# Scaling a tile inside the product that turns it: a diagonal of reciprocal norms in place of a VectorE pass

## What is computed

```python
h = rmsnorm(x, attn_norm)                    # y = x * rsqrt(mean(x*x) + eps) * gain
proj = h @ w_in                              # 1024 x 3584
o_a = dilated_mixture_attn(...)              # three groups of heads, dilations 1, 4, 16
o_b = sink_swa_gqa(...)                      # window of 128 with sinks
o_m = memory_attn(m_q, mem, mem_norm, ...)   # rmsnorm(mem) @ w_mem_kv, then attention
gates = sigmoid(h @ w_gate + b_gate)
merged = sum of gates[i] * (o_i @ w_o_i)
x = x + merged @ w_out                       # called x1 below
x = x + conv_ffn(rmsnorm(x, ffn_norm), w_up, conv_w, conv_b, w_down)
```

## Time and profile before

| | us |
|---|---|
| median of 3 runs | 1708.54 |
| lowest and highest | 1705.82, 1713.55 |
| the profiled execution | 1709.16 |
| its span in the trace | 1707.4 |
| PE busy | 1648.7 (97%) |
| DVE busy | 927.6 (54%) |
| POOL busy | 968.6 (57%) |
| ACT busy | 664.9 (39%) |
| mean granted clock of PE | 0.993 |

### The profile page before, as it was taken

One profiled execution on the slowest core, in us unless ns is written; L12 is line 12 of the kernel. 1 busy time (PEld: TensorE's weight loads), 2 busy tenths in 40 slices (PEclk: granted clock), 3 DMA queues, 4 the chain that ended last, 5 costly groups with the idle time before them and its releaser, 6 DMA issues.

```text
span 1707.4 us, 22529 instructions
## 1 busy us (share of the span) xinstructions
PE 1648.7 (97%) x8518; PEld 1353.1 (79%) x8518; DVE 927.6 (54%) x1327; ACT 664.9 (39%) x1172; POOL 968.6 (57%) x729
## 2 busy tenths in 40 slices
PE   7999989989899989999999999999999999999999
PEld 5887878868778768888888887788888888788887
DVE  7455342457875672224554367888888888522001
ACT  5555565545544333335212325343343434322110
POOL 5643656542312477775245548999999997222221
PEclk9999999999999999999999999999999999999999
DMA  5113011111110323332655502222222322443311
GB/s 219 38 59 103 2 38 41 38 26 33 44 38 8 86 80 114 121 100 77 182 158 183 191 38 62 87 84 89 75 74 87 94 80 103 163 146 128 140 50 62
DMA packets 132904, 151.07 MB, mean 88 GB/s; under 512 B 15349, under 2 KB 95933, under 8 KB 132797
## 3 DMA queue, kind: packets, MB, share of 16 engines
q1 hardware_dynamic: 132364, 149.62, 27.4%
q10 hardware_dynamic: 432, 0.01, 0.0%
HBM read 116.98 MB, written 32.62 MB: 88 GB/s over the span
## 4 chain that ended last, share of the span: by engine, by line
PE 59%; POOL 3%; DVE 2%; DMA 1%; ACT 1%; issue 0%; SPq 0%; DVEq 0%; ACTq 0%; POOLq 0%
PE ps L2805 24%; PE ps L2890 13%; PE ps L2140 11%; PE ps L2180 6%; PE ps L2196 3%; PE ps L2131 1%; DMA w_raw<-in_w_out_dram 1%; POOL wo L1862 1%; POOL f_lo L2646 0%; PE ps L2189 0%; DVE ffn_area L2763 0%; POOL f_lo L1867 0%; DVE attn_lo L2755 0%; DVE t_all L2673 0%; POOL ffn_area L1880 0%
## 5 line engine op out<-in xcount | busy, mean ns | idle before, releaser
L2646 POOL TENSOR_TENSOR f_lo<-ffn_area,f_hi 128x1024 fp32r<-128x1024 f32 x85 | 200.8, 2382 | 20.3 <-ACT f_hi L2533 20.3
L2678 POOL TENSOR_TENSOR attn_lo<-ffn_area,attn_lo 128x512 fp32r<-128x512 f32 x44 | 58.5, 1330 | 194.4 <-ACT attn_lo L2595 194.3
L2805 PE MATMUL ps<-t_all,f_hi 128*128 128x512 f32 x528 | 164.1, 392 | 1.9 <-DVE t_all L2673 1.6
L2533 ACT ACTIVATE f_hi<-ffn_area 128x1024 fp32r<-128x1024 f32 x85 | 80.2, 946 | 188.8 <-PE ps L2805 178.4
L1867 POOL TENSOR_TENSOR f_lo<-ffn_area,f_hi 128x1024 fp32r<-128x1024 f32 (+1 forms) x42 | 99.9, 2381 | 73.6 <-ACT f_hi L1715 73.6
L2805 PE MATMUL ps<-act_hi,f_hi 128*128 128x512 f32 x336 | 133.3, 397 | 4.6 <-POOL f_lo L2646 4.6
L688 POOL TENSOR_SCALAR head_rstd<-head_ss 128x8 f32<-128x8 f32 (+2 forms) x42 | 11.0, 262 | 217.9 <-DVE head_ss L979 217.9
L2805 PE MATMUL ps<-act_hi,f_lo 128*128 128x512 f32 x336 | 132.3, 394 | 0.0
L2805 PE MATMUL ps<-act_lo,f_hi 128*128 128x512 f32 x336 | 131.2, 391 | 0.0
L1277 PE MATMUL ps<-w_hi,act_hi 128*128 128x512 f32 (+1 forms) x320 | 122.5, 383 | 5.3 <-DVE w_lo L504 2.6
L2805 PEld LDWEIGHTS ps<-t_all,f_hi 128*128 128x128 f32 x528 | 98.9, 188 | 24.5 <-DVE t_all L2673 1.6
(11 more groups left out here) (314 smaller groups left out, 4586.5 us busy)
## 6 DMA issues: line engine op xcount, KB each, us to landing
ffn_area<-in_w_up_dram SPq DMA_DIRECT2D x44, 512.0 KB, 5.2
gate<-gates SPq DMA_DIRECT2D x24, 512.0 KB, 3.7
ffn_area<-in_w_gate_dram SPq DMA_DIRECT2D x23, 512.0 KB, 5.2
z<-attn_out SPq DMA_DIRECT2D x22, 512.0 KB, 2.6
ffn_area<-in_w_down_dram SPq DMA_DIRECT2D x22, 512.0 KB, 4.1
ffn_area<-z SPq DMA_DIRECT2D x44, 256.0 KB, 2.9
gates<-ffn_area SPq DMA_DIRECT2D x40, 256.0 KB, 2.1
attn_out<-in_x_dram SPq DMA_DIRECT2D x16, 512.0 KB, 6.3
```

The source lines that it names most:

```text
L2533: act.activation(part_place(p, part, f_hi, first_hi), part_source(p, part), ACT.Copy).then_inc(w_hi_done, 1)
L2646: pool.tensor_tensor(part_place(p, part, f_lo, first_lo), part_source(p, part), part_place(p, part, f_hi, first_hi).bitcast(F32), ALU.subt ...
L2678: pool.tensor_tensor(z_lo[:, m % 2, :], z_raw[:, m % 4, :], z_hi[:, m % 2, :].bitcast(F32), ALU.subtract).then_inc(z_lo_done, 1)
L2805: ins = pe.matmul(out, w, a, start=(start and k == 0 and i == 0), stop=(stop and k == 3 and i == 2))
```

## The change

The scaled tile is no longer written. DVE multiplies the unit matrix by the reciprocal norms, each row by its own, which gives a diagonal matrix of 128x128; for x and the memory it goes to a new tile `x_diagonal`, for x1 to the first 128 columns of the buffer in which the scaled tile stood. PE multiplies the unscaled tile as stationary operand by this diagonal as the moving one, in a plain float32 product in place of the transpose: the result is the turned tile with each column scaled. `x_diagonal` exists once, so its next writing waits until both halves of the tile before are turned (`x_turned`), the first one for `ident_ready`. The order of the instructions on every engine is the same as before: PE and DVE have as many, in the same places.

```diff
+        x_diagonal = sb("x_diagonal", [P, P])
...
             def x_scale(n):
                 dve.wait_ge(x_rstd, n + 1)
-                dve.tensor_scalar(x_slot[n], x_slot[n], row_rstd[:, n:n + 1], None, ALU.mult).then_inc(x_scaled, 1)
+                if n >= 1:
+                    dve.wait_ge(x_turned, 2 * n)
+                else:
+                    dve.wait_ge(ident_ready, 1)
+                dve.tensor_scalar(x_diagonal[:], ident[:], row_rstd[:, n:n + 1], None, ALU.mult).then_inc(x_scaled, 1)
...
                 for k in range(4):
-                    ins = pe.transpose(x_half(n, h)[:, k * P:(k + 1) * P], x_slot[n][:, (4 * h + k) * P:(4 * h + k + 1) * P],
-                                       ident[:])
+                    ins = pe.matmul(x_half(n, h)[:, k * P:(k + 1) * P], x_slot[n][:, (4 * h + k) * P:(4 * h + k + 1) * P],
+                                    x_diagonal[:], start=True, stop=True)
                 ins.then_inc(x_turned, 1)
...
                 dve.wait_ge(x1_rs, 2 * t + 2)
-                dve.tensor_scalar(staged[:, t % 2, :], x1[:, t, :], rstd[:, t:t + 1], None, ALU.mult).then_inc(x1_scaled, 1)
+                dve.tensor_scalar(staged[:, t % 2, 0:P], ident[:], rstd[:, t:t + 1], None, ALU.mult).then_inc(x1_scaled, 1)
...
                 for k in range(NK):
-                    ins = pe.transpose(turned(t)[:, k * P:(k + 1) * P], staged[:, t % 2, k * P:(k + 1) * P], ident[:])
+                    ins = pe.matmul(turned(t)[:, k * P:(k + 1) * P], x1[:, t, k * P:(k + 1) * P], staged[:, t % 2, 0:P],
+                                    start=True, stop=True)
                 ins.then_inc(x1_turned, 1)
```

## The result

The changed kernel takes **1720.39 us** (median of 6 runs, 1718.14 to 1721.74), the kernel before 1709.14 us in the runs beside it (6 runs, 1705.82 to 1713.55): a ratio of **1.0066, 95% interval 1.0053 to 1.0078**, slower by 11.25 us. The prediction was 1721.3 us (1716 to 1727) and slower. Other traces of the same two programs have spans of 1706.6 and 1707.0 us (before) and 1715.5 us (after), so a step of the ledger that is under 1 us can be chance where nothing else bears it out.

A forecast was written before the change was run, and what follows sets the result against it. PE, busy 97% of the span, was taken as the bound. Terms 0.8 + 0.9 - 0.1 - 1.5 + 5.5 + 7.1 gave +12.7 us, so 1721.9, lowered 0.6 to the median: 1721.3 us, range 1716 to 1727.

The forecast's parts named there:

- The price: Every turn on PE: a tile's eight plain products take 1.70 us against 0.79 for transposes, 0.91 us more.
- tiles 4 to 9: Half turns of x and the memory from 41.54 to 110 us: six times 0.91, +5.5 us.
- Rival C: All turns: plain products cost four times the transpose, 2.37 us more a tile, +40 us, 1749 us; chance 0.03.
- rival D: All turns: diagonal product costs PE what a transpose does, leaving only DVE's gain, 1707 us; chance 0.05.
- Tile 0: Kernel's start: slower first turn, partly hidden by ACT's square, delays the first projection and the w_lo wait; +0.8 us.
- Rival A: Near 18 us: w_lo slips ahead of POOL, removing the 2.2 us wait and half clock; 1717.6 or 1716.6; chance 0.12.
- Tile 1: Turn between 18 and 22 us: full price paid, half-clock stretch assumed to last as long; +0.9 us.
- Tiles 2 and 3: Ahead of the key copy at 41.54 us: PE's extra work fits into its wait; -0.1 us instead of +1.8.
- The clock behind the key copy: PE's half clock from 43 to 46 us goes as waits shrink; -1.5 us, bounds 0 and -1.5.
- x1: Eight x1 turns at 0.91 us, less a 0.2 us wait: +7.1 us, nothing hiding the last turn.
- Rival B: Clock does not recover: +14.2 us, 1722.8, or 1724.7 with nothing hidden at tiles 2 and 3; within forecast's 0.80.
- DVE's gain in all: Scalings of 18 tiles: 0.5 us less each, 9 us of DVE in all, almost none on the path.

The follow-up runs named there:

- x alone: Kernel before with only x and the memory scaled by the diagonal product, x1 left as it was; 1713.29 us, 1.0024.
- DVE alone: Kernel before with DVE making only the small diagonals, while PE transposes unscaled tiles and the multiplication by the norms is left out; 1704.91 us, 0.9978.
- tiles 1 to 3: Kernel before with the diagonal product for tiles 1, 2 and 3 of x only; 1709.76 us, 1.0001.
- the second repeat of the kernel before: Kernel before, unchanged, run again for a third trace; 1708.84 us.
- x1 alone: Kernel before with only x1 scaled by the diagonal product, x and the memory left as they were; 1713.56 us, 1.0031.
- one with doubled transposes: Kernel before with each transpose of the first x tile done twice, two traces: 1712.08 us with the early half-clock stretch, 1708.76 us without; the latter is meant.
- tile 0's four: Kernel before, two traces each: first x tile turned by plain unit-matrix products (1712.31, 1709.37 us), or its transposes done twice (1712.08, 1708.76 us).
- PE alone: Kernel before with every turn a plain product with the unit matrix, DVE's full scaling kept; 1721.58 us, 1.0079.

## Why the prediction held, point by point

**The price.** 0.91 us a tile was right where PE has no wait. In the chain of the x1 tiles each turn takes 1.78 us where it took 0.87, and tiles 4 to 9 shift the rest by 5.4 us for a forecast of 5.5. The chain of waits of the changed kernel at both ends of x1 (start us, us, what):

```profile
964.58 1.78 PE ps L2194 x16
...
1039.15 1.80 PE ps L2194 x16
...
1040.97 1.24 DVE ffn_area L2090
...
1042.23 0.69 DVE attn_out L2529
...
1046.76 3.33 DVE t_all L2679
...
1050.13 3.02 PE ps L2811 x12
```

Rival C (four times, 1749) and rival D (no price, 1707) have fallen with it, C by the time, D by the records and by the plain products with the unit matrix, which cost 0.79% with DVE's work unchanged.

**Tile 0.** Forecast +0.8, measured +0.55 at tile 1. The first projection comes 1.0 us later, a little more than I gave it. The second gain ends 1.37 us later (11.50 for 10.13, forecast 11.4) and ACT's high half starts 0.98 us later (11.54 for 10.56), so some 0.4 us are hidden behind the square, as said. What I had wrong is the wait for w_lo. I took it as following the same chain, but in DVE's order the scaling of tile 1 stands in front of w_lo, and I put its gain at nothing. Diagonal and w_lo together took 1.88 and 2.60 us, where scaling and w_lo had 2.34 and 2.56: 0.42 us less, and the wait shrank by 0.43, from 2.16 to 1.73 us. All 14 traces bear this out: from PE's first projection to its product behind w_lo it is 4.40 or 4.41 us in the five with a diagonal for tile 1 (both of the changed kernel, x alone, DVE alone, tiles 1 to 3), and 4.84 or 4.85 us in the nine others. Rival A had this at its core (the small operation makes w_lo come sooner beside POOL), but as a jump of 2.2 us; it was 0.4.

**Tile 1, the step that failed.** I assumed that the half-clock stretch of 19 to 22 us stays and lasts as long, and put +0.9. It is gone, and the step is -0.83. Four traces that transpose tile 1 and have no stretch here (the second repeat of the kernel before, x1 alone, DVE alone, one with doubled transposes) take 7.82 to 7.85 us from the turn of tile 1 to that of tile 2, the trace before 9.12 and the changed kernel 8.29 (8.45 in its second trace). So the clock gave 1.3 us, and the turn cost 0.45 to 0.6 us, not 0.9. Rival A would have had the stretch gone, because the wait goes. But the repeats of the kernel before show that the stretch is no fixed part of it at all: with a wait of 2.1 to 2.2 us it was there in two traces of three. So one trace was too little to put a sign on this term, and that the forecast stayed in its range without it is in part luck. Over the 14 traces of this case the stretch is there in 5 of the 8 with a wait of at least 2.1 us and in 1 of the 6 with at most 1.7 us. One of these six hardly counts: in x1 alone the wait is 0.7 us only because PE went at half its pace in front of it. Whether the shorter wait is the cause is suggested by these numbers at most, and not shown.

**Tiles 2 and 3.** Forecast -0.1, measured -0.18. PE's waits in the changed kernel, 0 to 60 us (total us, times, longest; before: 2.2 and the earlier trace rows):

```profile
PE ps L1282 <- DVE w_lo L505: 1.7, 1, 1.7
PE ps L1238 <- DVE k_ring L1030: 0.8, 1, 0.8
```

The wait for the key copy took up most of the two turns, as said, but from 1.9 us it went to 0.8 and not under 0.6. DVE's gain here was sized right: with the smaller operation alone the turn of tile 4 starts at 38.13 us, 1.9 us ahead of the one trace of the kernel before that also lacks the early stretch (39.99). 0.8 us of that are there at tile 1 already (17.72 for 18.49), where I had 0.5 and w_lo adds 0.4, and 1.1 us come at the key copy, where I had 1.0.

**The clock behind the key copy.** Forecast -1.5, "the least sure term", measured -1.5. It is also the one that the runs bear out best. In all eight traces where PE waits 1.9 us for the key copy (the three of the kernel before, the change in x1 alone, tile 0's four) a half-clock stretch follows between 40 and 48 us. In the six where it waits 0.8 to 1.6 us (both of the changed kernel, x alone, PE alone, DVE alone, tiles 1 to 3) none follows. With DVE's part alone, whose turns are as long as before, the two half turns of tile 4 stand 4.07 us apart for 5.60: 1.5 us for the clock. Rival B has fallen.

**x1.** Forecast +7.1, measured +5.9. Seven turns gave 5.9 instead of 6.2. The last one was the mis-sized one: I wrote that nothing hides it. DVE's gain behind it does start 10.5 us later (1030.43 to 1040.97), but the product that waits for the sums only 9.6 us. In between DVE's first sum took 1.62 us before, beside POOL's t_all of 3.50 us, which ran from 1029.26 to 1032.76:

```profile
1031.69 1.62 DVE attn_out L2523
...
1037.15 3.31 DVE t_all L2673
...
1040.51 3.02 PE ps L2805 x12
```

In the changed kernel POOL's t_all was over at 1042.06, before the sum at 1042.23, and that took 0.69 us. So the 0.93 us that the sum is shorter take back the last turn's 0.91: DVE reached it later, and POOL was no longer in its way. In x alone the sum (at 1033.21) takes 1.63 us; in x1 alone 0.69 us (at 1040.14): the cover comes with the change in x1.

**Behind x1** I had nothing, and the trace has +0.8. It lies between 1046 and 1100 us, in a longer stretch at a lower clock behind PE's 4.6 us wait for POOL, a wait that both kernels have. The average clock of that stretch is 0.97 before (1046 to 1100) and 0.94 after (1055 to 1110). That this belongs to the change is not borne out: the second repeat of the kernel before also has 0.94 there (1046 to 1100), and the second trace of the changed one 0.97 (1053 to 1110). Taken as the clock's loss over the whole span (one minus the granted clock, summed), the kernel before lost 12.3 to 14.9 us in three traces and the changed one 13.6 and 8.5 in two. This variation is about as large as the spread of the runs of one kernel.

**DVE's gain in all.** Forecast 9 us, measured 6.3 in the two groups. Undisturbed the operation takes 0.28 us for my 0.25. Four of the eighteen (1.88, 2.43, 2.41 and 1.31 us) run beside POOL, where the kernel before had three (2.34, 2.89 and 1.77): each of the three places gained 0.5 us, but the operation at 48.7 us, undisturbed before (0.75), newly fell beside POOL and takes 2.43. What counted was where it lies: the run of DVE's part alone has 4.0 us at the end. It is made of about 1.2 us at tile 1 (17.72 for 18.89; 0.5 of it from the scaling of tile 0, 0.4 from w_lo) and more at the key copy with the clock behind it, which here recovers as in the changed kernel. In my sum the clock's 1.5 us stood as a term of its own and 1.5 us as DVE's, together 3.0 of these 4.0.

**The sum.** Tile 0 -0.25, tile 1 -1.7, x1 -1.2, small ones and the end +0.9 against the forecast: 12.7 became 10.4 in the two profiled executions. By the medians it is 11.25, 1.45 less than the forecast; that the predicted time was only 0.9 us too high comes from the kernel before, whose median of six runs is 0.6 us above that of the first three.

## What to carry to other kernels

A multiplication that is folded into a transpose by putting the factors on a diagonal is not free on TensorE: in float32 it turns one record into two and 0.79 us into 1.70 us for eight blocks of 128x128. It can pay only where TensorE waits for just that scaling, so weigh it against TensorE's busy share stage by stage; here it was 97%. Even at the three tiles where it looked free the time did not change.
Before a stretch at half the clock is counted in a sum, take several traces of the kernel before: one that follows a wait of 1.9 us was there every time, one behind 2.2 us only in some.
And where the last delayed operation feeds an engine that shares its time with another, look at what runs beside each step after the shift, not only before.

## What the runs showed of the hardware

- **The clock fell again and again at the same few places**, each time behind a wait of PE, for some 3.4 us at half (about 1.7 us of work lost), at a few places for 6.8 us; but not in every execution. With a wait of 0.8 to 1.6 us at the key copy it never fell (6 traces), with 1.9 us always (8), yet near 18 us with 2.1 to 2.2 us in 5 of 8, and once with 1.74 us; in x1 alone it fell once, at 157 us, behind two waits of 0.9 and 0.6 us. Near 18 us the stretch cost 1.3 us of time. The length of the wait alone doesn't decide it.
- **The pace rose with nothing but transposes before it, though not each time.** In the kernel before tile 0's eight transposes take 1.97 us, about half the rate of the later ones (1.03), and behind them and the dummy transposes the projection at 12.91 us already has its full rate (0.50 us for the first product, 0.23 us from the second to the third). The Trainium skill, "TensorE: Matmul & The Clock Gate", "Part 4: PE-mode transpose", says of its clock gate that it does not engage for transpose mode. By this trace the rate did rise, and nothing but transposes had run before 12.91 us. So it is in six of the eight traces that transpose tile 0; in the second repeat of the kernel before it rose within the projection, and in x1 alone the projection went at half the rate, 0.43 us from start to start, up to 16.6 us:

```profile
13.64 0.63 PE L1277 MATMUL ps<-w_lo,act_hi 128*128 128x512 f32 x1
14.06 0.63 PE L1277 MATMUL ps<-w_hi,act_lo 128*128 128x512 f32 x1
```

  The column of the granted clock shows 1.00 for the slow 1.97 us too, so for this first stretch I go by the pace of the records.
- **DVE beside POOL waits, whatever the size of its operation.** The diagonal of 128 columns takes 0.28 us alone and 1.88 us at 13.77; the scaling of 1024 columns 0.75 us alone and 2.34 in the same place. Making it eight times smaller gained 0.5 us in both cases, and the wait of about 1.6 us stayed.
